# Router of a mixture of experts: counted top two, token rows on VectorE, expert loop written out

## The reference, cut to what matters

```python
h = rms_norm(x, ffn_norm[layer])
logits = (t @ router).astype(jnp.float32)          # t is h as (256, 1024)
top_vals, top_idx = lax.top_k(logits, TOP_K)       # the lower index wins a tie
gates = jax.nn.softmax(top_vals, axis=-1)
combine = jnp.sum(one_hot(top_idx, N_EXPERTS) * gates[..., None], axis=1)
for e in range(N_EXPERTS):                         # 8 experts, inner width 3584
    y = y + combine[:, e:e + 1] * swiglu(t, w_in[e], w_out[e])
```

## Time and profile before

| what | value |
|---|---|
| median of 3 runs | 1569.99 us |
| profiled execution, device time | 1570.96 us |
| its span, first to last instruction | 1569.2 us |
| PE busy | 1513.6 us, 96% |
| PE weight loads | 1276.2 us, 81% |
| DVE busy | 1199.7 us, 76% |
| ACT busy | 994.5 us, 63% |
| POOL busy | 127.1 us, 8% |
| mean granted clock of TensorE | 0.986 of full speed |
| DMA, mean over the span | 272 GB/s |
| POOL builds `span` and `lmask` | from 44.8 to 81.8 us |
| loads of 1 MB of expert input weights | 5.7 us from issue to landing, median |

### The profile page before, as it was taken

The page is one execution under the profiler, slowest core; times in us unless marked ns, Lnnn a source line. Parts: engine busy times, 40 slices in busy tenths (PEclk is TensorE's granted clock), DMA queues, the critical chain, the costliest instruction groups (busy, mean ns, idle before and its releaser), DMA issues.

```text
span 1569.2 us, 21897 instructions
## 1 busy us (share of the span) xinstructions
PE 1513.6 (96%) x8223; PEld 1276.2 (81%) x8223; DVE 1199.7 (76%) x1033; ACT 994.5 (63%) x855; POOL 127.1 (8%) x192
## 2 busy tenths in 40 slices
PE   6999999999999699999999999999998999999998
PEld 6967999989997478888888877888887888888886
DVE  6966544565485768888888888888987888888887
ACT  5657433465545567776776676677776677677774
POOL 8900000000152300000000000000000000000000
PEclk9979999999999899999999999999999999999999
DMA  9503655546500369999999999999998999999994
GB/s 302 188 1 120 210 183 186 186 149 200 184 32 21 127 242 368 336 366 341 348 360 345 348 340 335 355 346 360 354 341 323 340 347 364 347 343 366 346 364 163
DMA packets 205346, 426.88 MB, mean 272 GB/s; under 512 B 6737, under 2 KB 56074, under 8 KB 205242
## 3 DMA queue, kind: packets, MB, share of 16 engines
q1 hardware_dynamic: 204880, 424.78, 76.6%
q0 software_dynamic: 320, 0.69, 0.2%
q10 hardware_dynamic: 42, 0.01, 0.0%
HBM read 424.41 MB, written 1.05 MB: 271 GB/s over the span
## 4 chain that ended last, share of the span: by engine, by line
PE 68%; DVE 2%; ACT 1%; issue 1%; DVEq 0%; ACTq 0%
PE bank L1287 20%; PE bank L1288 20%; PE bank L1289 20%; PE bank L1541 2%; PE bank L1647 2%; PE bank L1618 1%; DVE w_l L275 1%; PE bank L1523 0%; PE bank L1522 0%; PE bank L1631 0%; PE bank L1630 0%; ACT w_h L270 0%; PE bank L1554 0%; DVE h_l L511 0%; PE bank L1564 0%
## 5 line engine op out<-in xcount | busy, mean ns | idle before, releaser
L275 DVE TENSOR_TENSOR w_l<-raw,w_h 128x2048 fp32r<-128x2048 f32 x403 | 922.0, 2291 | 259.1 <-ACT w_h L270 258.1
L270 ACT ACTIVATE w_h<-raw 128x2048 fp32r<-128x2048 f32 x403 | 772.8, 1918 | 404.3 <-PE bank L1289 402.3
L1287 PE MATMUL bank<-w_h,hs_h 128*128 128x512 f32 x896 | 359.5, 401 | 6.5 <-issue 2.6
L1288 PE MATMUL bank<-w_l,hs_h 128*128 128x512 f32 x896 | 353.5, 395 | 3.7 <-issue 3.7
L1289 PE MATMUL bank<-w_h,hs_l 128*128 128x512 f32 x896 | 353.8, 395 | 0.0
L1287 PEld LDWEIGHTS bank<-w_h,hs_h 128*128 128x128 f32 x896 | 168.1, 188 | 45.2 <-issue 3.0
L1289 PEld LDWEIGHTS bank<-w_h,hs_l 128*128 128x128 f32 x896 | 168.0, 187 | 44.9 <-issue 4.1
L1287 PE MATMUL bank<-h_h,w_h 128*128 128x256 f32 x672 | 193.0, 287 | 6.3 <-DVE h_l L511 6.3
L1288 PEld LDWEIGHTS bank<-w_l,hs_h 128*128 128x128 f32 x896 | 168.3, 188 | 37.9
L1288 PE MATMUL bank<-h_l,w_h 128*128 128x256 f32 x672 | 191.1, 284 | 0.0
L1289 PE MATMUL bank<-h_h,w_l 128*128 128x256 f32 x672 | 191.0, 284 | 0.0
(11 more groups left out here) (275 smaller groups left out, 1413.0 us busy)
## 6 DMA issues: line engine op xcount, KB each, us to landing
raw<-in_moe_w_in SPq DMA_DIRECT2D x224, 1024.0 KB, 5.7
raw<-in_moe_w_out SPq DMA_DIRECT2D x112, 1024.0 KB, 5.5
raw<-in_ffn_w_in SPq DMA_DIRECT2D x22, 1024.0 KB, 5.1
raw<-in_hgrn_w_in SPq DMA_DIRECT2D x16, 1024.0 KB, 5.5
raw<-in_ffn_w_out SPq DMA_DIRECT2D x11, 1024.0 KB, 4.9
raw<-in_ab_w_in SPq DMA_DIRECT2D x10, 1024.0 KB, 11.7
raw<-in_ab_w_out SPq DMA_DIRECT2D x4, 1024.0 KB, 5.0
raw<-in_hgrn_w_out SPq DMA_DIRECT2D x4, 1024.0 KB, 4.9
```

The source lines that it names most:

```text
L270: act.activation(w_h[:, u0 % S, :], raw[:, u0 % R, :], ACT.Copy).then_inc(w_high, 1)
L275: eng.tensor_tensor(w_l[:, u0 % S, :], raw[:, u0 % R, :], w_h[:, u0 % S, :], ALU.subtract).then_inc(w_low, 1)
L1287: pe.matmul(o, a_high, b_high, start=start, stop=False, skip_group_check=True)
L1288: pe.matmul(o, a_high, b_low, start=False, stop=False, skip_group_check=True)
```

## The change

1. **Token rows.** The product of row scale and gain row moves from POOL to one DVE instruction on `x` (`token_rows`), inside `residual_norm(3)`. The two remainders move to DVE as well (`token_rest`, `token_low`), the first pair around the logit steps, the second pair between the selection masks and the rank table. ACT rounds the high and middle parts ahead of `split_high(U_MOE + 2)`.
2. **Top two by counting.** Every logit is compared with the 8 of its token (128 elements in a partition), once by "greater" and once by "greater or equal"; a predicated copy takes the second where the other expert comes earlier; a sum gives each expert's place. A place under 1.5 is chosen.
3. **Ranks.** The masks are bf16 (`chosen`, padded to 64 columns for a token half), `before_b` and `ones_b` too. Two products of 128 columns give both halves' ranks, a third the counts for `flag`. Slot numbers start at 1, so one instruction forms the rank table. Dummy products (`keep_warm`) stand before (8) and after (3).
4. **Later work.** `split_low(U_MOE + 1)` moves behind `choose`, `split_low(U_MOE + 2)` behind `gather_low`, and the gates (`gates`) behind that; ACT takes the exponential and the load of the Silu table behind `gather_high` and ahead of `split_high(u + 3)`.
5. **Experts written out.** In the first pass the 8 experts are straight code on all five engines.
6. **Memory.** `span` and `lmask` share memory with the tensors of the first layer, so POOL builds them only after the first part of that layer's output product (`o_part`). POOL makes two more small constants early on.

```diff
+        earlier = sb("earlier", [P, TT, NE, NE], I8)
-        span = sb("span", [P, 5, 2, P], F32R)
-        lmask = sb("lmask", [P, 7, P], I8)
...
+            if r == 0:
+                for e in range(NE):
+                    expert(e, e, 0, e % 2, e == NE - 1)
+                return
...
+            pool.wait_ge(o_part, 1)
             step(pool.memset(span[:].bitcast(F32), 1.0))
...
-            for tt in range(TT):
-                pool.wait_ge(n_xn, 2 * (TT * 3 + tt) + 2)
-                pool.tensor_tensor(x_g[:, tt, :], xn[:, tt, :], gain_row[:], ALU.mult).then_inc(x_gain, 1)
-            for part in range(2):
-                for tt in range(TT):
-                    pool.wait_ge(x_part, 2 * part + tt + 1)
-                    dst = x_g[:, tt, :] if part == 0 else x_b[:, 2, tt, :]
-                    pool.tensor_tensor(dst, x_g[:, tt, :], x_b[:, part, tt, :], ALU.subtract).then_inc(x_gain, 1)
...
+            def token_rows(tt):
+                dve.wait_ge(gain_in, 16)
+                dve.scalar_tensor_tensor(out=x_g[:, tt, :], in0=x[:, tt, :], scalar=n_stat[:, 3, 4, tt:tt + 1], in1=gain_row[:],
+                                         op0=ALU.mult, op1=ALU.mult).then_inc(x_gain, 1)
+            def token_rest(tt):
+                dve.wait_ge(x_high, tt + 1)
+                dve.tensor_tensor(x_g[:, tt, :], x_g[:, tt, :], x_b[:, 0, tt, :], ALU.subtract).then_inc(x_gain, 1)
+            def token_low(tt):
+                dve.wait_ge(x_mid, tt + 1)
+                dve.tensor_tensor(x_b[:, 2, tt, :], x_g[:, tt, :], x_b[:, 1, tt, :], ALU.subtract).then_inc(x_low, 1)
...
-            split_low(dve, U_MOE + 1)
-            split_low(dve, U_MOE + 2)
+            token_rest(0)
...
             dve.tensor_copy(logit_t[:], bank[0:NE, 4, 0:T]).then_inc(r_lc, 1)
+            token_rest(1)
...
+            mine = logit[:, 0, :, :].unsqueeze(3).to_broadcast([P, TT, NE, NE])
+            other = logit[:, 0, :, :].unsqueeze(2).to_broadcast([P, TT, NE, NE])
+            dve.tensor_tensor(above[:, 0, :, :, :], other, mine, ALU.is_gt).then_inc(r_d, 1)
+            step(dve.tensor_tensor(above[:, 1, :, :, :], other, mine, ALU.is_ge))
+            step(dve.copy_predicated(above[:, 0, :, :, :], earlier[:], above[:, 1, :, :, :]))
+            step(dve.tensor_reduce(logit[:, 1, :, :], above[:, 0, :, :, :], AX.X, ALU.add))
+            step(dve.tensor_scalar(chosen[:, 1:3, 0:NE], logit[:, 1, :, :], 1.5, None, ALU.is_lt))
             n_const["sel"] = done[0]
+            token_low(0)
+            token_low(1)
             dve.wait_ge(r_rank, 1)
+            step(dve.scalar_tensor_tensor(out=rank[...], in0=bank[:, 4, 0:P]..., scalar=1.0,
+                                          in1=chosen[:, 1:3, 0:NE], op0=ALU.add, op1=ALU.mult))
...
                 choose(0, r, 0)
+                    split_low(dve, u + 1)
+                    dve.wait_ge(r_rank, 2)
...
                 gather_low(n0, 0)
+                if r == 0:
+                    split_low(dve, u + 2)
+                    gates()
...
                 gather_high(n0, 0)
+                if r == 0:
+                    act.wait_ge(r_d, n_const["exp"])
+                    act.activation(pick[:, 5, :], pick[:, 4, :], ACT.Exp).then_inc(r_e, 1)
+                    table(ACT.Silu)
                 split_high(act, u + 3)
...
+            keep_warm(8, 7)
             pe.wait_ge(r_d, n_const["sel"])
-            pe.matmul(bank[:, 4, 0:NE], before[:], s0, start=True, stop=True)
...
+            pe.matmul(bank[:, 4, 0:P], before_b[:], chosen[:, 1:3, :], start=True, stop=False)
+            pe.matmul(bank[:, 4, 0:P], ones_b[:], chosen[:, 0:2, :], start=False, stop=True).then_inc(r_rank, 1)
+            pe.matmul(bank[:, 3, 0:P], ones_b[:], chosen[:, 1:3, :], start=True, stop=True).then_inc(r_rank, 1)
+            keep_warm(3, 7)
```

More of the change, by code:

```diff
@@ L94, in build @@
         ident = sb("ident", [P, P])
-        ones = sb("ones", [P, P])
         mean_all = sb("mean_all", [P, P])
         mean_64 = sb("mean_64", [P, P])
-        before = sb("before", [P, P])
+        before_b = sb("before_b", [P, P], BF16)
+        ones_b = sb("ones_b", [P, P], BF16)
+        earlier = sb("earlier", [P, TT, NE, NE], I8)
         slot_no = sb("slot_no", [P, 2, P])
@@ L308, in _ @@
                 pool.dma_start(router[:], A["moe_router"][0].rearrange("(c p) e -> p c e", p=P)).then_inc(rout_in, 16)
-            step(pool.memset(ones[:], 1.0))
+            step(pool.memset(ones_b[:], 1.0))
             step(pool.memset(mean_all[:], 1.0 / P))
@@ L321, in _ @@
             step(pool.memset(conv_in[:, :, 0:TAPS - 1], 0.0))
-            step(pool.memset(before[:], 1.0))
-            select(before[:], [[1, P]], -1, -1)
+            step(pool.memset(before_b[:], 1.0))
+            select(before_b[:], [[1, P]], -1, -1)
+            step(pool.memset(earlier[:], 1))
+            select(earlier[:], [[0, TT], [1, NE], [-1, NE]], -1, 0)
             for r in range(2):
-                step(pool.iota(slot_no[:, r, :], pattern=[[1, P]], base=CAP * r, channel_multiplier=0,
+                step(pool.iota(slot_no[:, r, :], pattern=[[1, P]], base=CAP * r + 1, channel_multiplier=0,
                                allow_small_or_imprecise_dtypes=True))
@@ L790, in _ @@
                 split_low(dve, u + 3)
+            dve.memset(chosen[:], 0.0).then_inc(r_pad, 1)
             residual_norm(3)
             norm_low(3, C_FFN + 8)
-            split_low(dve, U_MOE + 1)
-            split_low(dve, U_MOE + 2)
+            token_rest(0)
             done = [0]
@@ L839, in _ @@
-            step(dve.tensor_scalar(rank[:].rearrange("p (a e) -> p a e", a=TT)[:, :, 0:NE], logit[:, 9, :, :], -1.0, None, ALU.add))
+            mine = logit[:, 0, :, :].unsqueeze(3).to_broadcast([P, TT, NE, NE])
+            other = logit[:, 0, :, :].unsqueeze(2).to_broadcast([P, TT, NE, NE])
+            dve.tensor_tensor(above[:, 0, :, :, :], other, mine, ALU.is_gt).then_inc(r_d, 1)
+            done[0] += 1
+            step(dve.tensor_tensor(above[:, 1, :, :, :], other, mine, ALU.is_ge))
@@ new lines, in gates @@
+            def gates():
+                for k in range(2):
+                    step(dve.tensor_scalar(logit[:, 4 + k, :, :], logit[:, 1, :, :], float(k), None, ALU.is_equal))
+                step(dve.tensor_reduce(pick[:, 0, :], logit[:, 0, :, :], AX.X, ALU.max))
+                step(dve.scalar_tensor_tensor(out=logit[:, 3, :, :], in0=logit[:, 4, :, :], scalar=-3.0e38, in1=logit[:, 0, :, :],
+                                              op0=ALU.mult, op1=ALU.add))
+                step(dve.tensor_reduce(pick[:, 1, :], logit[:, 3, :, :], AX.X, ALU.max))
+                step(dve.tensor_tensor(pick[:, 4, :], pick[:, 1, :], pick[:, 0, :], ALU.subtract))
+                n_const["exp"] = done[0]
+                dve.wait_ge(r_e, 1)
+                step(dve.tensor_scalar(pick[:, 6, :], pick[:, 5, :], 1.0, None, ALU.add))
+                step(dve.reciprocal(pick[:, 7, :], pick[:, 6, :]))
+                step(dve.tensor_tensor(pick[:, 8, :], pick[:, 5, :], pick[:, 7, :], ALU.mult))
+                step(dve.tensor_tensor(logit[:, 7, :, :], logit[:, 4, :, :], wide(pick[:, 7, :]), ALU.mult))
+                step(dve.tensor_tensor(logit[:, 8, :, :], logit[:, 5, :, :], wide(pick[:, 8, :]), ALU.mult))
+                step(dve.tensor_tensor(comb[:].rearrange("p (a e) -> p a e", a=TT)[:, :, 0:NE], logit[:, 7, :, :], logit[:, 8, :, :], ALU.add))
@@ L1199, in _ @@
             norm_high(3, C_FFN + 8)
-            split_high(act, U_MOE + 2)
-            for part in range(2):
-                for tt in range(TT):
-                    act.wait_ge(x_gain, 2 * part + tt + 1)
-                    act.activation(x_b[:, part, tt, :], x_g[:, tt, :], ACT.Copy).then_inc(x_part, 1)
-            act.wait_ge(r_d, n_const["exp"])
-            act.activation(pick[:, 5, :], pick[:, 4, :], ACT.Exp).then_inc(r_e, 1)
+            for tt in range(TT):
+                act.wait_ge(x_gain, tt + 1)
+                act.activation(x_b[:, 0, tt, :], x_g[:, tt, :], ACT.Copy).then_inc(x_high, 1)
+            for tt in range(TT):
+                act.wait_ge(x_gain, TT + tt + 1)
+                act.activation(x_b[:, 1, tt, :], x_g[:, tt, :], ACT.Copy).then_inc(x_mid, 1)
+            split_high(act, U_MOE + 2)
+            table(ACT.Exp)
             def gather_high(n, b):
@@ L1260, in moe_round @@
                 n0, s0 = r * NE, r * NE * MOE_STEPS
-                act.activation(m_silu[:, 0:1], eps[:], ACT.Silu)
                 if r:
+                    act.activation(m_silu[:, 0:1], eps[:], ACT.Silu)
                     for i in range(3):
```

65 lines of the change are left out of this document (23 added, 42 removed).

## The result

The changed kernel took 1556.4 us, the median of 4 runs (1554.27 to 1556.85), against 1570.4 us for the kernel before (4 runs, 1569.7 to 1572.36): a ratio of 0.9906, 95% interval 0.9889 to 0.9923. It is faster, but by 14 us where 20.4 were forecast, and the time lies above the forecast range. Of all executions behind this document one, of the kernel with only the straight experts, took 2199.14 us at a mean granted clock of 0.637; it is left out of that kernel's median and ratio.

A forecast was written before the change was run, and what follows sets the result against it. PE was taken as the bound in the experts, with DVE's chain holding it in the router. Loop 9.7 + router 10.7 (11.5 - 0.8) = 20.4 us off 1569.99 gives 1549.6 us; whole range 1546.5 to 1555.

The forecast's parts named there:

- Experts written out: Expert loop: straight code removes two back edges of 4.89 and 4.77 us, together 9.7 us; ends 0 and 9.7.
- both mechanisms: Loop: straight code has no back edge. Router: DVE's small steps no longer stand still until an instruction of POOL has ended.
- Router up to the gather: Router, DVE's chain: masks at 534.4 instead of 544.0, PE's gather starting at 537.5 instead of 547.50, 10.0 us earlier.
- The gather: PE's first gather: dummies cut idle gaps to 2 us or less, so 2.65 instead of 4.53 us, -1.9 us.
- the clock stays low through the gather: Rival at PE's gather: gaps around the dummies still enough; +1.9 less 0.4 hidden by DVE's lateness, 1551.1 us; chance 0.10.
- DVE's lateness behind the gather: Before the first expert unit: DVE does `split_low(u+1)` and the `flag` count ahead of `gather_low`, adding 0.4 us.
- The wait for u+3: Early in expert 0: unit u+3 needs the gates through, so PE waits once; taken as 0.8 us, ends 0 and 2.5.
- no drain: At ACT's Silu table load: none shows in the trace; one would lengthen the u+3 wait by 1.4 us; larger-wait rival 0.07.
- The move of the masks in memory: `span` and `lmask`: about 37 us of POOL work moves after 139, needed near 415; no cost forecast for their addresses.
- None of the rivals on record: Rivals: low gather clock 0.10, larger u+3 wait 0.07, slow compares 0.05, transfers taking back the loop's gain 0.05, instruction fetch 0.03.
- The masks' new time on POOL: Beside the second norm and dense layer: moved mask building taken to cost 0 us, ends 0 and 1.
- its sentence on two inputs: Second norm: DVE with two SBUF inputs contends with GpSimd reading SBUF, the later standing still; up to 1 us, taken 0.

## Why the prediction was wrong

The direction and both mechanisms were right. The sum came out 5.9 us too large, and the step that failed is a term put at nothing without a reason: what the new place of the masks in memory does to the experts' products. It measured 3.9 us. A second one, the gather's clock, was mis-sized by 1.8 us.

- **Experts written out: right.** 9.7 us were forecast. From the first copy of `scat` to the eighth it was 885.3 us and is 879.0 (628.09 to 1507.12). The 6.2 us between them are the 9.66 of the edges less 7 x 0.49 for the longer experts. Alone, straight code gave 10.6 us on the median. One reading was off: of PE's four gaps at the edges (2.58, 1.86, 2.48 and 1.84 us) three are labelled issue, and the third is put down to DVE's `w_l`. It went with the edges like the others.
- **Router up to the gather: right.** 10.0 us forecast, 10.03 measured (547.50 to 537.47), and 10.1 from the start of the low feature parts in each trace (20.83 to 10.73). The steps on DVE took 0.29 + 0.29 + 0.30 + 0.28 in place of the 0.35 each. Restoring POOL's part gave the slow steps back.
- **The gather: wrong.** 2.65 us forecast, 4.47 measured. This was the rival "the clock stays low through the gather", given 0.10, with the 1.5 us that it named; the kernel with 12 dummies shows 1.6. The forecast put 8 dummies beneath `token_low`. Eight of the eleven are issued ahead of the masks (531.98, 1.90 us); only three, 0.81 us, lie beneath it, and PE is idle for 2.10 us just ahead of the gather. That placing is what failed. Of the 1.8 us 1.6 are the clock; 0.2 stay without it (2.84 against 2.65). The 0.4 us that the forecast added for DVE's lateness behind the gather did not come: it is 1.4 us from the gather's end to the first unit, as before, in this kernel and in the one with 12 dummies. So 1.4 us are missing at the first unit.
- **The wait for u+3: right.** 0.8 us forecast, 0.56 measured (552.60, for DVE's `w_l`), once. The exponential ended at 546.83 and the table load began at 546.85: no drain.
- **The move of the masks in memory: the step that failed.** The prediction costed `span` and `lmask` by the time of POOL only, and their place in memory at nothing. Together with the new tensors of the router it moved the experts' tensors from 96 to 224 modulo 256, and their products slowed by 0.49 us x 8 = 3.9 us. Two thirds of the missing 5.9 are this. The kernel with only that memory change and the ones with 128 and 4992 bytes of pad show it from both sides. None of the rivals on record was this one.
- **The masks' new time on POOL: small, but not 0.** In the second norm the two multiplications on DVE now lie beside POOL's selects. Their timeline after:

```profile
143.72 1.42 DVE L491 TENSOR_SCALAR xn<-x,n_stat 128x512 f32<-128x512 f32 x2
...
147.04 1.06 DVE L491 TENSOR_SCALAR xn<-x,n_stat 128x512 f32<-128x512 f32 x2
```

and with the masks held back until the norm is through:

```profile
143.45 0.88 DVE L493 TENSOR_SCALAR xn<-x,n_stat 128x512 f32<-128x512 f32 x2
...
146.25 0.88 DVE L493 TENSOR_SCALAR xn<-x,n_stat 128x512 f32<-128x512 f32 x2
```

The transposes behind the scaling, and with them the first dense product, come 0.5 us later for it (149.08 to 149.56); the kernel with only the memory change has the same 1.42 and 1.06. I had read from the earlier trace rows that POOL is always the one that waits. The two rows do not even lie beside each other: the four selects end at 51.98 and the split starts at 53.34, beside later ones. All that they show is a split that was hardly slowed. The Trainium skill, "SBUF — State Buffer", section "Who interferes with whom", also says that a `tensor_scalar` can enter a mode with two ports, when its operands meet the conditions, and that DVE in such a mode contends with GpSimd. I had weighed only its sentence on two inputs. These rows agree with it: 0.88 us becomes 1.42 and 1.06. It was about cancelled by 0.4 us gained in front of the router, where in the kernel before POOL's multiplication stood beside the same pair of scalings (1.32 us at 524.34, and 0.88 now, at 524.74).
- **The end:** from ACT's last copy to the end it is 47.58 us, and was 46.88. Of these 0.7 us 0.2 are the slower products up to the first store of the result. The other 0.5 lie between that store's issue and the end, 6.61 us where it was 6.08. In the twelve kernels with straight experts it is 6.4 to 7.0, in the four with the loop 6.1 to 6.4, so it seems to go with the straight code. Why is open.

Together: 10.1 (all up to the first unit) + 9.7 (edges) - 3.9 (offset) - 0.6 (u+3) - 0.5 (end) = 14.8, against 14.5 measured. 0.3 us are unassigned.

**Where executions of one kernel differ.** The first layer took 129.9 to 133.1 us over all these kernels, whatever its code. The window from 84 to 90 us of the changed kernel:

```profile
84.00:90.00 6.00, 6.00 (x16) 3.03 (x16) 3.69 (x10) 3.42 (x18) 0.00 (x0) 0.50 0.00 0
```

and of the one with 12 dummies, identical up to there:

```profile
84.00:90.00 6.00, 6.00 (x19) 2.96 (x18) 4.60 (x11) 3.95 (x20) 0.00 (x0) 0.68 0.00 0
```

PE does light work there, at a clock of 0.50, and in the second execution the clock fell later, so that the mean over these 6 us is 0.68. That is probably most of the 1.8 us between the two (132.71 and 130.87 us, from the first weight product to the first dense one). The moment differs from execution to execution, and so a stage is compared by its own length; where times of day stand above, as for the gather, the lengths give the same (10.1 beside 10.03).

## What to carry to other kernels

When an edit adds, removes or moves a tensor in SBUF, write down where the operands of the hot products land before and after; put the stationary and the moving operand at the same offset modulo 256 bytes, and check the products' mean time on the page, since no wait will show it. This is measured for float32 products of 128x128 by 128x512 alone; the gain there was 20.8 us in one kernel and 21.1 in another. Work that fills PE to keep its clock must reach right up to the work that it protects: with a gap of 2.1 us just ahead it was lost, and dummies issued after the clock has fallen cost double. On DVE, keep instructions with two SBUF inputs away from POOL's: 0.3 us becomes 2.

## What the hardware showed that I had not expected

- The pace of full matmuls of 128x512 depends on the offsets of their operands in SBUF. Level modulo 256, an expert takes 122.5 to 122.8 us; at differences of 32 or 128 bytes (96 and 0 against 128) 125.3; with 224 against 128, 125.8. By the page's groups, the product of `w_h` and `hs_h` took 396, 401 and 403 ns on the mean. Between the first and the last period lie 2.4%; in the kernel before, 32 bytes of pad are worth 20.8 us.
- Which of the two fetches is slowed isn't known. A unit smaller than 256 doesn't fit: offsets that differ by 128 (0 and 128, 96 and 224) give different periods. 0, 96, 128 and 224 are all that was tried, and only for these shapes. Shapes of other layers react too. The dense layer took 192.65 us or 193.6 to 193.8, the recurrence 52.5 to 53.0 us or 53.9 to 54.1, depending on the pads; their offsets were not varied by themselves, so a layout good for every layer remains to be found. In the dense layer the difference between the operands orders the times as well: weights less activations (`act_h`) modulo 256 is 64 in the nine kernels with 192.65 or 192.66 us, 192 in those with 193.55 to 193.58, 32 in two with 193.61, and 160 in two with 193.77, one of which has the weights at 128 and the other at 0. 160 is the slowest difference in the experts too. No kernel had that layer level.
- A back edge costs 4.7 to 7.0 us in these traces: 4.89 and 4.77 in the kernel before, 5.10 and 4.74 in it with only the memory change, 5.4 and 6.9 in it with the 32 byte pad, and 5.4 and 7.0 with the new router. So the router is not what makes it dearer. What does is open.

The best version measured is the changed kernel with 12 dummies, the held-back masks and the level operands: 1530.97 us, ratio 0.9738 (0.972 to 0.9756), against 0.9906 for the change as it was given.
